# Hymba layer on one core: low parts of the FFN weights by VectorE, or by adding transfers

## The reference

```
h2 = rmsnorm(x, ffn_norm_w[l])
x = x + (jax.nn.silu(h2 @ w_gate[l]) * (h2 @ w_up[l])) @ w_down[l]
```

## Time and profile before

| | us |
|---|---|
| median of 3 runs | 2516.64 (2516.51 to 2516.84) |
| span of the profiled execution | 2514.7 |
| PE busy | 2481.1 (99%) |
| VectorE busy | 1074.2 (43%) |
| ACT busy | 805.6 (32%) |
| GpSimd busy | 116.2 (5%) |

### The profile page before, as it was taken

One profiled execution on the slowest core, in us unless ns is written; L12 is line 12 of the kernel. 1 busy time (PEld: TensorE's weight loads), 2 busy tenths in 40 slices (PEclk: granted clock), 3 DMA queues, 4 the chain that ended last, 5 costly groups with the idle time before them and its releaser, 6 DMA issues.

```text
span 2514.7 us, 31129 instructions
## 1 busy us (share of the span) xinstructions
PE 2481.1 (99%) x12009; PEld 2030.2 (81%) x12009; DVE 1074.2 (43%) x1534; ACT 805.6 (32%) x1160; POOL 116.2 (5%) x151
## 2 busy tenths in 40 slices
PE   6999999999999999999999999999999999999998
PEld 5777777788888788888888888888888888888886
DVE  6766666663334444523333333324242424232334
ACT  5544444443334432422222222222222222222225
POOL 3111111110000000000000000000000000000000
PEclk9999999999999999999999999999999999999999
DMA  5322222222233323333323332333333233333322
GB/s 160 97 67 67 67 67 67 67 67 68 83 84 83 148 86 117 88 97 101 100 85 98 100 92 91 100 100 87 97 100 99 84 100 100 84 99 100 97 87 100
DMA packets 326698, 231.60 MB, mean 92 GB/s; under 512 B 4128, under 2 KB 293504, under 8 KB 325248
## 3 DMA queue, kind: packets, MB, share of 16 engines
q1 hardware_dynamic: 325792, 224.72, 30.5%
q10 hardware_dynamic: 864, 6.29, 0.6%
HBM read 226.81 MB, written 4.19 MB: 92 GB/s over the span
## 4 chain that ended last, share of the span: by engine, by line
PE 92%; DVE 4%; issue 2%; ACT 1%; DMA 1%; SPq 0%; POOL 0%; DVEq 0%; ACTq 0%; POOLq 0%
PE bank L1435 29%; PE bank L1437 28%; PE bank L1436 28%; PE bank L1564 2%; PE bank L1498 1%; PE bank L1674 1%; PE bank L1657 1%; DVE w_low L934 0%; DMA x<-in_x_dram 0%; DVE sq L1121 0%; PE bank L1633 0%; PE bank L1627 0%; PE bank L1431 0%; DMA raw<-in_w_in_dram 0%; ACT x L707 0%
## 5 line engine op out<-in xcount | busy, mean ns | idle before, releaser
L934 DVE TENSOR_TENSOR w_low<-raw,w_high 128x1024 fp32r<-128x1024 f32 x408 | 513.3, 1258 | 980.5 <-ACT w_high L553 980.3
L1435 PE MATMUL bank<-h_high,w_high 128*128 128x512 f32 x2176 | 871.4, 400 | 1.0 <-DVE w_low L934 1.0
L1437 PE MATMUL bank<-h_high,w_low 128*128 128x512 f32 x2176 | 849.6, 390 | 0.0
L1436 PE MATMUL bank<-h_low,w_high 128*128 128x512 f32 x2176 | 848.0, 390 | 0.0
L553 ACT ACTIVATE w_high<-raw 128x1024 fp32r<-128x1024 f32 x408 | 431.8, 1059 | 1219.9 <-PE bank L1437 1214.9
L1435 PEld LDWEIGHTS bank<-h_high,w_high 128*128 128x128 f32 x2176 | 408.7, 188 | 87.8 <-issue 2.4
L1437 PEld LDWEIGHTS bank<-h_high,w_low 128*128 128x128 f32 x2176 | 408.5, 188 | 87.5
L1436 PEld LDWEIGHTS bank<-h_low,w_high 128*128 128x128 f32 x2176 | 409.1, 188 | 78.4 <-issue 0.7
L1437 PE MATMUL bank<-w_high,hid_low 128*128 128x512 f32 x704 | 278.4, 396 | 0.0
L1436 PE MATMUL bank<-w_low,hid_high 128*128 128x512 f32 x704 | 278.4, 395 | 0.0
L1435 PE MATMUL bank<-w_high,hid_high 128*128 128x512 f32 x704 | 278.4, 395 | 0.0
(11 more groups left out here) (235 smaller groups left out, 1410.5 us busy)
## 6 DMA issues: line engine op xcount, KB each, us to landing
raw<-in_w_in_dram SPq DMA_DIRECT2D x57, 1024.0 KB, 5.6
raw<-in_w_gate_dram SPq DMA_DIRECT2D x44, 1024.0 KB, 5.6
raw<-in_w_up_dram SPq DMA_DIRECT2D x44, 1024.0 KB, 5.6
raw<-in_w_down_dram SPq DMA_DIRECT2D x44, 1024.0 KB, 5.0
raw<-in_w_out_dram SPq DMA_DIRECT2D x16, 1024.0 KB, 5.0
x<-in_x_dram SPq DMA_DIRECT2D x4, 1024.0 KB, 9.0
x<-in_x_dram ACTq DMA_DIRECT2D x4, 1024.0 KB, 8.0
out_dram<-x SPq DMA_DIRECT2D x8, 512.0 KB, 3.1
```

The costliest lines, as they stand in the source:

```text
L934: V.tensor_tensor(w_low[:, s % SLOTS, :], raw[:, (s // 2) % 2, (s % 2) * HALF:(s % 2 + 1) * HALF], w_high[:, s % SLOTS, :].bitcast(F32), A ...
L1435: M(out_ap, stat[0], mov[0], start=start, stop=False, skip_group_check=True)
L1436: M(out_ap, stat[0], mov[1], start=False, stop=False, skip_group_check=True)
L1437: return M(out_ap, stat[1], mov[0], start=False, stop=stop, skip_group_check=True)
```

## The change

In the loop over the groups 1 to 10, and only there, `w_low` is made another way. ACT writes the half twice, as `w_high` = rounded(raw) and, behind it, as `w_low` = rounded(-raw), which is the negated high part (`minus_high`). GpSimd then issues a transfer from `raw` to `w_low` with an accumulate operation, so that `w_low` becomes -high + raw. It waits until all 16 counts of that transfer are there, then for the turn of the half, and gives `w_low_ready` itself. VectorE's `low` is gone from the loop. The pieces ahead of the loop and behind it are as they were, with one new wait of VectorE for the last of GpSimd's halves.

```
+        w_minus_ready = sem("w_minus_ready")
+        w_low_added = sem("w_low_added")
+        w_minus_seen = sem("w_minus_seen")
...
+            with pool.Fori(1, FF_GROUPS) as n:
+                span = S_FF(n)
+                for j in range(24):
+                    s = span[0] + j + LEAD
+                    pool.wait_ge(w_minus_ready, 24 * n + (j + 1 - 24))
+                    pool.sem_inc(w_minus_seen, 1)
+                    pool.dma_start(w_low[:, s % SLOTS, :], raw[:, (s // 2) % 2, (s % 2) * HALF:(s % 2 + 1) * HALF],
+                                   accum_op=ALU.add).then_inc(w_low_added, 16)
+                    pool.wait_ge(w_low_added, 16 * 24 * n + 16 * (j + 1 - 24))
+                    pool.wait_ge(w_low_ready, count(span, j + LEAD))
+                    pool.sem_inc(w_low_ready, 1)
...
+            def minus_high(span, j):
+
+                s = span[0] + j + LEAD
+                A(w_low[:, s % SLOTS, :], raw[:, (s // 2) % 2, (s % 2) * HALF:(s % 2 + 1) * HALF], ACT.Copy, scale=-1.0
+                  ).then_inc(w_minus_ready, 1)
...
                 for j in range(24):
                     high(span, j)
+                    minus_high(span, j)
                     if j == 0:
                         hidden_high(n - 1, 3)
...
                         half_done(dve, span, -1)
                         product(n - 1, 3)
                         hidden_low(n - 1, 3)
-                    low(span, j)
                     if j in (4, 16, 20):
...
             hidden_low(FF_GROUPS - 1, 3)
+            dve.wait_ge(w_low_ready, count(S_END, LEAD))
             for j in range(8):
                 low(S_END, j)
```

## The result

| | before | after |
|---|---|---|
| median of the runs, us | 2516.59 (2516.51 to 2516.84) | 2925.95 (2925.44 to 2927.09) |
| span of the profiled execution | 2514.7 | 2924.6 |
| VectorE busy | 1074.2 | 791.6 |
| ACT busy | 805.6 | 1018.0 |

The ratio is 1.1627, with a 95% interval of 1.1613 to 1.1641: 16% slower, 409 us. Forecast were 2879 us, a loss of 362 us, within 2512 to 3720 us.

A forecast was written before the change was run, and what follows sets the result against it. PE was taken as the bound at 5.49 us per half, GpSimd's serial additions as the new one at 1.9 + 3.9 + 0.8 + 0.4 = 7.0 us: 362 us lost over 240 halves, 2879 us, range 2512 to 3720 us.

The forecast's parts named there:

- The bound and the period: In the FFN loop PE bounds at 5.49 us per half; removing VectorE's 295 us of work is worth 0.
- ACT's copies: ACT in the loop: 240 negated copies of 1061 ns each, 255 us more, hidden, worth 0.
- The mechanism: GpSimd's queue in the loop: 240 additions form one serial chain; above 5.49 us per half it bounds, 362 us lost.
- C: Time between GpSimd's signals, forecast 7.0 us; also a rival: adding slow in the DMA engines, past 10.5 us, chance 0.13.
- The terms of C: Per addition on GpSimd's chain: 1.9 us independent of size, 3.9 moving, 0.8 sharing, 0.4 GpSimd's own steps, 7.0 us together.
- The sharing: DMA engines in the loop: raw loads and additions dispute about 1 us per half, counted as 0.8 us.
- One of the forecast's own signs: Additions' landing time minus the store's gives the price of adding; at 4.3 us or less, 3.9 us moving is wrong.
- B: Rival in GpSimd's loop: addition costs one more full-rate read, 5.4 us per half, hidden; 2516.6 us, chance 0.19.
- The second read: Skill pages on an addition: 2.0 us plus 2.4 us for bytes with a second read, 4.4 us, under the period.
- D: Rival, raw loads bound the loop: landing in 12 us instead of 5.5, 132 us lost, 2649 us, chance 0.07.
- The clock: PE in the loop: waiting 1.5 us per half does not lower its clock to 1.2 GHz; worth 0.
- "Evenly spaced" and PE waiting 240 times: Sign in the loop: additions evenly spaced, PE's first matmul of each half waiting some 1.5 us, 240 times.

The follow-up runs named there:

- e7: Changed kernel without its additions: GpSimd waits for ACT's negated copy and gives the signal; 2516.78 us, ratio 1.0000 to the kernel before.
- e5: Changed kernel, but GpSimd only waits for copies and issues; PE and SP wait for the additions' own semaphores, one per slot; 2516.77 us, ratio 1.0000.
- e3: Changed kernel with the loop's loads moving 64 KB instead of 1 MB each; 2522.7 us in its one run.
- e8: Changed kernel with plain transfers of raw to w_low instead of additions; 2562.88 us in its one run.
- e9: e2 with SP's load also waiting until PE has done two of four chunks of the half; 2603.48 us, ratio 1.0348.
- e4: Changed kernel with additions for the even halves alone, the others by VectorE as before; 2516.58 us, ratio 1.0000.
- e2: Changed kernel with a third buffer for raw in the loop, additions still one at a time; 2924.42 us, ratio 1.1624.
- e6: e5 with a third buffer for raw, so that a load goes out a unit earlier; 2516.86 us, ratio 1.0001.
- e1: Changed kernel with two additions in flight: GpSimd issues the next before it waits for the one ahead; 2848.48 us, ratio 1.1318.

## Why the prediction was right, and where it was wrong

**The bound and the period.** Right. PE was the bound, the period 5.49 us per half, and removing VectorE's work gave 0 (e7).

**ACT's copies.** Right: 1041 ns each, hidden (e7).

**The mechanism.** Right. GpSimd's queue is a serial chain, and the loss is 240 x (C - 5.49), with C = 7.2 us for a forecast 7.0; e5 takes away the wait for the landing, with the signal behind it, and the loss is 0.

**The terms of C.** Right only in the sum, which is luck. The moving was put at 3.9 us, by the rate of the raw loads; it is 2.77 us (e3). 1 MB read in 2.77 us is 379 GB/s, near the full rate of the earlier trace rows, the end of my bounds that I had not taken. What doesn't depend on size, with GpSimd's steps, was put at 2.3 us; it is 5.35 - 2.77 = 2.6 us (a remainder; no run splits it). The sharing was put at 0.8 us; it is (9.03 - 5.35) / 2 = 1.8 us. The first is 1.1 us too high, the other two together 1.3 us too low. The plain transfer of e8 bears out the middle term: 3.70 - 1.44 = 2.3 us, and 0.33 us more for the dearer issue of an addition. One of the forecast's own signs showed: landing minus the store's is 4.6 - 3.1 = 1.5 us alone and 3.2 us in the median of all (6.3 us on the page), under 4.3 us, so the 3.9 us of moving were too many, and yet B was not right, because of the sharing.

**The failed step** is the sharing. The prediction had the load fall somewhere among the additions and disputed half of it. But SP's load and GpSimd's next addition are released by the same signal, so they collide every time and nearly all of the load's 3.9 us lands on the chain. The diff and the waits say this before any run; I read the two waits on one count, wrote "both are late with it", and did not ask what they do together when released. e9 shows that it is the moment that counts.

**The second read.** My estimate from the Trainium skill's "DMA: Bandwidth & Descriptors" (Anatomy of one DMA) and "Collectives: The Full Stack" (The bandwidth ceiling) was 4.4 us from issue to landing. The runs agree: 4.6 us in e4 where nothing is beside, and a plain transfer moves for 52% of the time of an addition (e8). What the estimate leaves out is GpSimd's 0.75 us between a landing and its next issue, and the loads.

**Rival B**, the cover holds with C = 5.4 us: this was near only by chance to what an addition alone costs, 5.35 us, since B's sum holds 0.7 us for the loads. Both of its parts were too low: the addition alone, 4.7 for 5.35 us, and above all the loads, 0.7 for 1.8 us. **C** is excluded by e3. **D**, the loads as the bound, is excluded by e2, although ACT waits some 1090 us for them.

**The clock.** Wrong in the step, but it was worth nothing, as forecast. I wrote that PE would wait 1.5 us per half and keep 2.4 GHz. The wait comes bunched, once per two halves. PE stops at about 1917.7 us and starts again at 1921.1 us, with the granted clock still at 1.00. It falls to 0.50 (1.2 GHz) at about 1922.2 us, when PE is at work again, and is back at 1.00 by 1925.7 us. After the stop before, from 1904.0 to 1906.5 us, it stayed at 1.00. The mean is 0.962. The forecast called a wait of 1.5 us far from the more than 4 us at 1.00 behind PE's last matmul in the earlier trace rows. But those rows show only that the fall comes later than the stop. It does here too, some 4.5 us behind it, and by then PE had started again.

That the slower stretches cost nothing can be read from the trace. A turn goes from GpSimd's issue behind a long interval to the next such issue, two additions later; 115 turns of 1150 to 2850 us can be cut out so. The 38 turns whose mean granted clock is below 0.9 last 14.39 us in the median, the 39 at 1.00 last 14.41 us. GpSimd's chain sets the pace, and PE only waits less when it works more slowly.

**"Evenly spaced" and PE waiting 240 times** were wrong for the same reason as the sharing: the intervals alternate, and the row of PE's waits has 114 of them, up to 3.7 us.

No version beat the kernel before; e4, e5 and e6 equal it. PE leaves nothing in the loop for any of them to win.

## What to carry to other kernels

When a transfer replaces an engine's instruction, price the chain from one issue to the next, and not its latency: a wait for the landing in the issuing queue makes latency into period. Then look for every transfer that the same signal releases, since these met each time here; holding the load back until it left 2.6 us behind an addition's issue, not 0.6 us ahead of it, was worth 321 us (e9), where another buffer gave nothing clear of the noise (e2). A long total of waits can name an engine that is early and not the bound; give it room, as e2 does, before you believe it.

## What the runs showed of the hardware that was not expected

- An adding transfer SBUF to SBUF of 128 rows of 4 KB lands in 4.5 to 4.7 us when nothing is beside it (e4). It occupies the 16 engines for 2.77 us (e3), a plain one that goes through GpSimd for 1.44 us (e8), and GpSimd itself for 0.86 against 0.53 us.
- Beside a load of 1 MB the addition's interval grows by 3.7 us, about all of the load's own 3.9 us, though the two are on different queues. Each transfer is slower in a crowd (a load 11.1 us instead of 5.5 in e1), but the engines did carry 85% load without loss (e5).
- PE's granted clock fell to a half about 4.5 us after PE had stopped, though PE had been at work again for 1.1 us, and stayed there until 1925.7 us; a wait of 2.5 us one turn earlier had left it at 1.00. At the end of the kernel before it fell between 2508.0 and 2508.5 us, where PE had stopped at about 2503.4 us. In both places the fall came more than 4 us after the stop, so a low clock in a row need not belong to a wait in that row. Which of the waits in the loop lower it stays open.
